# Sparse attention with the value operand widened from 65 to 128 columns

## What is computed

```python
# selected blocks: per query the blocks in ix, causal inside them
s = einsum('bqgrd,bgqnld->bgrqnl', qi, kg) * scale
p = softmax(where(mask, s, NEG))
o_s = einsum('bgrqnl,bgqnld->bqgrd', p, vg)
# window
s_w = einsum('bcqgrd,bckgd->bcgrqk', qb, kb) * scale
p_w = softmax(where(mask_w, s_w, NEG), axis=-1)
o_w = einsum('bcgrqk,bckgd->bcqgrd', p_w, vb)
o = g[..., 0, :] * o_c + g[..., 1, :] * o_s + g[..., 2, :] * o_w
```

## Time and profile before

| | us |
|---|---|
| median of 3 runs | 5622.82 |
| lowest, highest | 5592.83, 5622.99 |
| span of the profiled execution, first to last instruction | 5558.8 |
| sparse attention stage, within the span | 4190 to 4619.5 |

### The profile page before, as it was taken

The page is one execution under the profiler, slowest core; times in us unless marked ns, Lnnn a source line. Parts: engine busy times, 40 slices in busy tenths (PEclk is TensorE's granted clock), DMA queues, the critical chain, the costliest instruction groups (busy, mean ns, idle before and its releaser), DMA issues. The chain is left out here.

```text
span 5558.8 us, 89699 instructions
## 1 busy us (share of the span) xinstructions
PE 4857.4 (87%) x38696; PEld 3782.4 (68%) x38718; DVE 2766.3 (50%) x3829; ACT 1117.0 (20%) x1625; POOL 702.8 (13%) x630
## 2 busy tenths in 40 slices
PE   9997997999798998574859979997886999999999
PEld 7776887988686766243437747765654557788887
DVE  5776543444445885473664476232563235433342
ACT  2443221222320330000011221111331112100010
POOL 0002321111000460000000011010000000141330
PEclk9998998999889998786978989998888789999999
DMA  3443113111213333514222244146003004212213
GB/s 135 161 160 113 48 29 117 57 57 59 101 45 131 125 137 144 187 67 152 76 72 109 76 133 136 59 121 167 16 22 78 5 8 145 95 46 80 79 42 103
DMA packets 240395, 513.00 MB, mean 92 GB/s; under 512 B 26935, under 2 KB 112248, under 8 KB 239364
## 3 DMA queue, kind: packets, MB, share of 16 engines
q1 hardware_dynamic: 177700, 363.19, 20.3%
q0 software_dynamic: 31488, 110.53, 5.8%
q10 hardware_dynamic: 30816, 33.56, 1.7%
HBM read 353.96 MB, written 150.74 MB: 91 GB/s over the span
## 5 line engine op out<-in xcount | busy, mean ns | idle before, releaser
L4645 PE MATMUL tail_product<-tail_x_hi,tail_w_hi 128*128 128x512 f32 x832 | 329.5, 396 | 11.8 <-DVE tail_x_lo L128 11.0
L4645 PE MATMUL tail_product<-tail_x_lo,tail_w_hi 128*128 128x512 f32 x832 | 325.3, 391 | 0.0
L4645 PE MATMUL tail_product<-tail_x_hi,tail_w_lo 128*128 128x512 f32 x832 | 324.7, 390 | 0.0
L3501 PE MATMUL win_product<-kept_hn_hi,win_w_hi 128*128 128x512 f32 x560 | 228.1, 407 | 39.9 <-DVE win_w_lo L128 39.9
L1741 PE MATMUL front_product<-kept_x_hi,front_w_hi 128*128 128x512 f32 x544 | 220.6, 405 | 10.7 <-DVE kept_x_lo L128 10.5
L3501 PE MATMUL win_product<-kept_hn_hi,win_w_lo 128*128 128x512 f32 x560 | 219.5, 392 | 0.0
L3501 PE MATMUL win_product<-kept_hn_lo,win_w_hi 128*128 128x512 f32 x560 | 219.3, 392 | 0.0
L1741 PE MATMUL front_product<-kept_x_hi,front_w_lo 128*128 128x512 f32 x544 | 213.5, 392 | 0.0
L1741 PE MATMUL front_product<-kept_x_lo,front_w_hi 128*128 128x512 f32 x544 | 213.1, 392 | 0.0
L3155 PE MATMUL lc_ps<-idft,lc_zz 128*128 128x256 f32 x512 | 120.2, 400 | 91.2 <-DVE lc_zz L3033 91.2
L4645 PE MATMUL tail_product<-tail_f_hi,tail_w_hi 128*128 128x512 f32 x480 | 189.7, 395 | 0.0
(11 more groups left out here) (737 smaller groups left out, 11739.3 us busy)
## 6 DMA issues: line engine op xcount, KB each, us to landing
s_decayed<-front_ring SPq DMA_DIRECT2D x96, 256.0 KB, 4.0
tail_w<-in_w_gu SPq DMA_DIRECT2D x44, 512.0 KB, 3.2
win_w<-in_w_in SPq DMA_DIRECT2D x35, 512.0 KB
front_w<-in_even_w SPq DMA_DIRECT2D x34, 512.0 KB, 4.0
win_cq_hi_plain<-in_ada_w POOLq DMA_DIRECT2D x16, 1024.0 KB, 5.4
dn_kv<-s_qkv SPq DMA_DIRECT2D x16, 768.0 KB, 6.6
kept_held<-s_decayed SPq DMA_DIRECT2D x4, 3072.0 KB, 14.6
rk_in<-s_decayed SPq DMA_DIRECT2D x4, 3072.0 KB, 16.5
```

Of the source, the lines that this page charges most:

```text
L3501: mm = pe.matmul(pp[:, u, h, :], l, b, start=(k == 0 and m == 0), stop=(k == depth(s) - 1 and m == 2))
L4645: mm = pe.matmul(pp[:, s % 2, h_, :], l, b, start=(k == 0 and m == 0), stop=(k == deep(s) - 1 and m == 2))
```

## The change

The value tile gets 128 columns for each key block and group, 64 values and 64 ones, and a head's product now has 128 columns, so that four heads fill the 512 columns of the bank. The view `sums` has a pitch of 128. VectorE still reads columns 0 to 63 as values and column 64 as the sum; the other 63 columns of ones give the same sum again and are read by nobody. The fill with ones covers columns 64 to 127. No instruction is added, removed or moved on any engine; the 912 records of L3970 change from 128x65 to 128x128.

```diff
@@ -3838,7 +3838,7 @@
     with Stage(nc, tag) as st:
         q = [st.sb(f"q{g}", [P, 4, T]) for g in range(2)]
         k = [[st.sb(f"k{x}{g}", [P, T]) for x in range(2)] for g in range(2)]
-        v = [st.sb(f"v{x}", [P, QB, 2, 65]) for x in range(2)]
+        v = [st.sb(f"v{x}", [P, QB, 2, P]) for x in range(2)]
@@ -3861,7 +3861,7 @@
         NMADE = 7
-        sums = lambda x: po[x][:, 0:260].rearrange("p (r c) -> p r c", c=65)
+        sums = lambda x: po[x][:, :].rearrange("p (r c) -> p r c", c=P)
         half_of = lambda b: b // 4
@@ -4068,7 +4068,7 @@
                 for x in range(2):
-                    dve.memset(v[x][:, :, :, 64:65], 1.0).then_inc(made, 1)
+                    dve.memset(v[x][:, :, :, 64:P], 1.0).then_inc(made, 1)
                 dve.memset(mq[:, :, :, :], 0.0).then_inc(made, 1)
```

## The result

| | before | after |
|---|---|---|
| median, us (10 runs each) | 5587.74 | 5535.99 |
| lowest to highest, us | 5548.13 to 5622.99 | 5529.7 to 5552.22 |
| ratio of the times, 95% interval | | 0.9925 (0.9903 to 0.9946) |
| span of the profiled execution, us | 5558.8 | 5535.3 |

The changed kernel is faster by 0.75%, some 42 us by the ratio and 52 us by the medians. By the 1% bound of the prediction that is "no change", as forecast; by its own interval it is a clear gain. The predicted gain was 36 us, but the predicted time of 5587 us was 51 us too high, and the range that began at 5560 did not hold the result.

What follows compares the result with a forecast made beforehand. TensorE, busy 87% of the span, was taken to bound the kernel. Four zero costs and 36.1 us gained from the clock sum to -36 us, carried to the 5622.82 us median: 5587 us, range 5560 to 5617.

Steps and rivals of the forecast that it cites:

- the 1% bound of the prediction: Whole kernel: changes within 1%, 56 us, count as no change; chances 0.83 within, 0.15 faster, 0.02 slower.
- The cost of the extra columns: Sparse attention's 912 value-product records: 128 columns fit under the 0.112 us pitch set by the weight load; cost 0.
- rival C: Value products: extra columns add to the pitch, 53 ns per record, 48 us slower, 5671 us; chance 0.04.
- Reciprocals, fills, loads: Sparse attention: later reciprocals, longer fills with ones and wider-stride value loads stay hidden; each costs 0.
- The mechanism: Sparse attention: twice the column work at the same pitch brings TensorE's full clock back sooner, worth 36.1 us; chance 0.62.
- Rival A: Sparse attention: the clock goes by something the extra columns do not touch; no change, 5623 us; chance 0.17.
- The way back: Sparse attention: each half-clock stretch ends with its first run of 16 value products, 7.7 and 16.1 us after the falls.
- I leave both falls in place: Sparse attention: the change adds nothing around the two clock falls, so both stay; 23.8 us at half clock remain.
- The sum against the span: Whole kernel: the 36 us gain taken from the profiled span of 5558.8 us gives 5523 us.
- I carry the difference over to the median: Whole kernel: the median, 5622.82 us, stands 64.0 us above the span; the gain applied to it gives 5587 us.
- 82.1 us go: Sparse attention: half-clock time that disappears, at 0.44 us for each us, worth 36.1 us.
- rival B: Sparse attention: the clock no longer falls or returns almost at once; 46.7 us gained, 5576 us, perhaps 5560; chance 0.17.

Runs made afterwards that it cites:

- layout kernels: Changed kernel's layout with products taking only 65 of the 128 columns: stage run eight times 8801.22 us; stage run once 5585.98 us, ratio 1.0011 to the kernel before.
- the 96 columns: Changed kernel with the attention stage run eight times, each product taking 96 of the 128 columns: 8516.38 us.
- the zeros: Changed kernel with the attention stage run eight times, columns 65 to 127 of the value tile zero instead of one: 8384.91 us.
- eight-fold changed kernel: Changed kernel with the sparse attention stage run eight times in a row instead of once: 8361.63 us.
- eight-fold kernel before: Kernel before the change with the sparse attention stage run eight times in a row instead of once: 8815.41 us.
- the added products: Changed kernel with the stage run eight times, plus five bf16 products of 512 columns ahead of each of 16 turn-backs per stage: 8378.74 us.

## Why the prediction was right and wrong

**The cost of the extra columns, 0: nearly right.** The pitch is 0.111 us, and rival C is out. The DeltaNet row of the same shape foretold it. What the sum left out is the first product of each run, whose columns do show: 3.3 us a stage. The prediction had the right size for it, 53 ns once for the last product of a group, but let only VectorE wait for it. The estimate from the Trainium skill ("TensorE: Matmul & The Clock Gate", "Back-to-back issue gap"), 24 us, did not come.

**Reciprocals, fills, loads, 0: right.** The reciprocals wait 76.6 us for the products, as long as before (77.8 us), and the fills lie in a wait.

**The mechanism: right.** The layout kernels, the 96 columns and the zeros leave only the columns streamed, through the clock. Rival A (no change) is out: TensorE was recorded busy for about the same share (347 of 377 us before, 330 of 355 after) and the clock still answered. The rule of the Trainium skill ("TensorE: Matmul & The Clock Gate", "The HAM clock gate (the "warmup" mystery)") says that the clock is set by how busy TensorE has lately been. If recorded busy time is meant, these runs do not agree: 110.15 of 114.50 us were recorded busy in the half stretch of 65 columns above that lasted to the end of its stage.

**The way back: right.** "I therefore let each half stretch end with its first run of 16 value products" is what all five half stretches of the changed profile do. In the eight-fold changed kernel, too, none that begins behind the first value product lasts over 17.1 us.

**"I leave both falls in place": right for the two, and they are not all.** Both are still there, at 232 and 448 value products. But the changed profile has five falls after the first value product, and 46.8 us at half clock where 23.8 were forecast. The fall at 472 was hidden inside the old half stretch. Those at 17 and 688 are places where the profiled execution of before was spared and others are not: in the eight-fold kernel before, two of the eight stages fall at 16 and 20, and four fall at 688. What decides where an execution is spared is not shown. Against its own profile of before the gain is therefore smaller than forecast: the stages, from the first value product on, are

```profile
4242.40:4620.30 377.90, 348.05 (x1966) 207.06 (x1985) 111.13 (x294) 70.39 (x87) 0.00 (x0) 0.86 0.02 5
```

before and

```profile
4241.00:4596.40 355.40, 330.23 (x1987) 195.03 (x1985) 110.83 (x294) 70.54 (x88) 0.00 (x0) 0.93 0.02 5
```

after, 22.5 us less, and the spans differ by 23.5 us. The sum against the span, 5523 us, would have been 12 us too low for that reason.

**"I carry the difference over to the median": the step that failed.** The prediction took the 64.0 us between the span and the median over whole, as if they were a fixed part of the time. They are not. The profiled execution of the changed kernel took 5537.08 us with a span of 5535.3 us, so 1.8 us lie outside the span. The profiled execution of before then took about 5560.6 us, 27.1 us under the median of ten runs, of which only one was lower. The other 35.1 us are the median of three runs over the median of ten: 1.8 + 27.1 + 35.1 = 64.0 us.

The 27 us are clock. The profiled execution's 105.9 us at half clock were a lucky draw: the eight stages of the eight-fold kernel have 107 to 226 us, 174 on the mean, and the luckiest of them falls at the same two places, 232 and 448. The single kernels say the same. For 31 other executions of the kernel before, the mean granted clock of each is known; time goes with half-clock time at 0.43 us per us, and the mean is 1015 us at half clock in the whole kernel, where the profiled execution has 946. The changed kernel has 896 on the mean of its ten. So 119 us go on the mean, worth 51 us; less 3.3 for the columns that is 48 us, and the means of the times differ by 47.5 us (5586.3 and 5538.8).

So two things went wrong at once. The baseline, the median of three runs, stood 35.1 us over the median of ten; and the term of the sum "82.1 us go" was mis-sized for a typical execution: 141 us go in an eight-fold stage and about 119 in the single kernel, which is worth 52 us by the medians (42 by the ratio), not 36. The 51 us by which the time was missed are these: 35.1 + (51.7 - 36.1) = 50.7 us. That the forecast of 36 us stands between the 23.5 us of the two profiles and the 52 us of the medians is luck: it took too little half-clock time for the kernel before, and too little for the changed one.

I had seen that the three runs lay 30 us apart and that one half stretch more or less is worth about that much. Having seen it, the range had to be as wide as that scatter on both sides, and the profile's place in it had to be an open question. Its lower end was also set loosely: by the prediction's own 24 us for a third half stretch, rival B reaches 5576 - 24 = 5552 us, not 5560. That would not have held the result either.

**Faster, same or slower:** the measured 0.75% lies within 1%, where 0.83 of the chance was put. Rival B, whose price was the whole 46.7 us, came nearest in size, but its mechanism did not come true: the clock does still fall. One stage of eight without a fall, at 335.9 us against 349.9 us on the mean, shows what it would be worth: 14 us more.

## What to carry over

Where a matmul's pitch is set by the weight load, columns added up to that pitch are nearly free: here they cost 0.055 us for each run of products. They bring the clock back sooner, and that is worth 0.75% of the kernel. Where TensorE bounds a stage, read the granted clock of its stretches, not only its busy share: here 0.41 to 0.44 us are lost for each us at half clock. And one profiled execution is one draw: if runs lie 30 us apart, repeat the stage some times in one kernel and read the spread before a number is carried from one draw to a median.

## What was not expected

The scatter of the times shrank with the change, from 75 us over ten runs to 23 us; the sparse attention stage was what made most of the difference between executions of this kernel, by up to 53 us in a single stage. With the layout alone the scatter stays, 58 us over twelve runs. Half-clock time could be cut further, to 7 us a stage, but in this stage it was not worth the work that it took. Half of the added products stood where there was no pause: a pause read at one turn-back does not stand for all sixteen.
